# A hybrid decoder layer on one core: inverse RMS moved to the outputs of the up product, with its operands built during a tile-by-tile output projection

## The reference, cut to what matters

```python
h = h + jnp.concatenate([y_conv, y_ret], axis=-1) @ w_out     # 1024 x 1024
hn2 = rmsnorm(h, norm_mlp)                                    # h * rsqrt(mean(h*h)) * gain
h = h + jnp.square(jax.nn.relu(hn2 @ w_up)) @ w_down          # 1024 x 4096, 4096 x 1024
```

## Time and profile before

| | us |
|---|---|
| median of 3 runs (1291.13 to 1292.31) | 1291.59 |
| the profiled execution, its own time | 1291.18 |
| its span, first to last instruction | 1289.4 |
| output projection, 402.9 to 512.3 | 109.4 |
| up product to the start of its last pass, 512.3 to 870.4 | 358.1 |
| last up pass and first down block, 870.4 to 972.5 | 102.1 |
| rest of the down product and the end, 972.5 to 1289.4 | 316.9 |

### The profile page before, as it was taken

One profiled execution on the slowest core, in us unless ns is written; L12 is line 12 of the kernel. 1 busy time (PEld: TensorE's weight loads), 2 busy tenths in 40 slices (PEclk: granted clock), 3 DMA queues, 4 the chain that ended last, 5 costly groups with the idle time before them and its releaser, 6 DMA issues. The chain is left out here.

```text
span 1289.4 us, 22653 instructions
## 1 busy us (share of the span) xinstructions
PE 1172.3 (91%) x8721; PEld 1142.0 (89%) x8721; DVE 730.2 (57%) x1061; ACT 480.7 (37%) x953; POOL 693.1 (54%) x660
## 2 busy tenths in 40 slices
PE   8999999999996998768999999995599999999876
PEld 7889999999996997768999999994499999999875
DVE  4355455455547467964444544443377777777545
ACT  5313214123143333544343434343344444444313
POOL 0144253242423628564646464643488889888972
PEclk9999999999998999879999999998799999999989
DMA  5331311212110543033434343436475455554303
GB/s 183 120 83 50 84 33 51 81 49 67 34 52 18 176 127 99 15 109 108 160 112 152 120 144 128 137 135 190 131 232 147 132 141 156 149 148 133 115 16 117
DMA packets 166125, 142.90 MB, mean 111 GB/s; under 512 B 6140, under 2 KB 133336, under 8 KB 166034
## 3 DMA queue, kind: packets, MB, share of 16 engines
q1 hardware_dynamic: 161262, 139.26, 35.1%
q10 hardware_dynamic: 4772, 2.40, 0.6%
HBM read 101.19 MB, written 40.46 MB: 110 GB/s over the span
## 5 line engine op out<-in xcount | busy, mean ns | idle before, releaser
L1692 PE MATMUL pair<-b_hi,up_hi 128*128 128x258 f32 x896 | 262.0, 292 | 59.0 <-DVE hid L1410 27.3
L1692 PE MATMUL pair<-m_hi,dn_hi 128*128 128x258 f32 x896 | 258.3, 288 | 25.2 <-DVE hid L1473 12.2
L1693 PE MATMUL pair<-b_lo,up_hi 128*128 128x258 f32 x896 | 259.2, 289 | 0.0
L1694 PE MATMUL pair<-b_hi,up_lo 128*128 128x258 f32 x896 | 259.1, 289 | 0.0
L1694 PE MATMUL pair<-m_hi,dn_lo 128*128 128x258 f32 x896 | 256.2, 286 | 0.0
L1693 PE MATMUL pair<-m_lo,dn_hi 128*128 128x258 f32 x896 | 255.7, 285 | 0.0
L1692 PEld LDWEIGHTS pair<-b_hi,up_hi 128*128 128x128 f32 x896 | 175.6, 196 | 63.6 <-issue 34.0
L1692 PEld LDWEIGHTS pair<-m_hi,dn_hi 128*128 128x128 f32 x896 | 172.2, 192 | 27.3 <-issue 14.1
L1499 PE MATMUL pair<-x_hi,w_both 128*128 128x344 f32 (+2 forms) x576 | 189.0, 328 | 0.3 <-DVE v L1128 0.3
L1500 PE MATMUL pair<-x_lo,w_both 128*128 128x344 f32 (+2 forms) x576 | 184.5, 320 | 0.0
L1501 PE MATMUL pair<-x_hi,w_both 128*128 128x344 f32 (+2 forms) x576 | 184.5, 320 | 0.0
(11 more groups left out here) (184 smaller groups left out, 2271.7 us busy)
## 6 DMA issues: line engine op xcount, KB each, us to landing
m_raw<-m_dram SPq DMA_DIRECT2D x56, 516.0 KB, 3.8
m_dram<-hid SPq DMA_DIRECT2D x14, 1548.0 KB, 6.4
up_raw<-w_up_dram SPq DMA_DIRECT2D x32, 512.0 KB, 5.0
dn_raw<-w_down_dram SPq DMA_DIRECT2D x128, 128.0 KB, 2.8
w_raw<-w_in_dram SPq DMA_DIRECT2D x28, 512.0 KB, 3.6
w_raw<-w_out_dram SPq DMA_DIRECT2D x16, 512.0 KB, 4.1
h_dram<-hid SPq DMA_DIRECT2D x16, 258.0 KB, 3.4
h_in<-h_dram SPq DMA_DIRECT2D x16, 258.0 KB, 4.2
```

What stands on the lines that cost most here:

```text
L1692: m_.matmul(to, shs[k], mhs[k], start=STARTS[i] and k == 0, stop=False, skip_group_check=more)
L1693: m_.matmul(to, shs[k], mls[k], start=False, stop=False, skip_group_check=more)
L1694: ins = m_.matmul(to, sls[k], mhs[k], start=False, stop=k == last, skip_group_check=more)
```

## The change

**What moves.** The operands of the up product are built from h times gain alone, without the inverse RMS. The inverse RMS, `r_all`, one row for all partitions, is multiplied to the outputs: DVE's `scaled` does max(x, 0) * r on the four finished blocks of a pass, ACT then only squares them. The relu on ACT goes.

**Output projection.** 16 groups (`SEQ_OUT`) of 48 matmuls, tile by tile over all columns; w_out is loaded and split once. Groups of tiles 0 to 3 take half 0 first, those of 4 to 7 half 1 first. After each group ACT and DVE build what has become complete: `first_block`, `combine` (the four block sums, one tile at a time, on DVE in the place of h itself), `op_split`/`op_rest` (splits tile by tile) and `square_sum` (now on DVE). POOL only adds the residuals, after the split of y (`ylo_done`), and forms sums of weights.

**Up product.** 16 whole passes. `mid_sum` moves from POOL to DVE (ahead of the next pass's step 1); POOL has `up_sum` alone, with a wait of its own for each of the four sums. In pass 0 the last operands (`block_split`/`block_rest` 3 and 5, `op_split`/`op_rest` 6) are built and the inverse RMS is made: row sums on PE after steps 0 and 1, root on one partition, then four transfers (to memory, back as 86 x 12, after the reciprocal to memory again, and to all partitions).

**Crossing to the down product.** `m_raw` lies where `m_lo` goes, one place for each of the seven loads of a block; a load waits for the products that used its place before, no longer for the splits of an earlier load. `mid_split` and `mid_low` stand later in the lists. In SP's list the loads of h stand behind the seven loads of block 0, and the store of the last pass is issued after the first down group's loads.

The core of the diff (waits and placements that the text doesn't speak of are left out):

```diff
-TILES = 2 * KT
-GROUPS = 2 * TILES
+SEQ_OUT = [(n, l) for n in range(KT) for l in ((0, 1) if n < 4 else (1, 0))]
+GROUPS = len(SEQ_OUT)
...
-UP = [(0, (0,)), (1, (0,)), (1, (1,)), (0, (1,))] + [(u, (0, 1)) for u in range(2, UNITS)]
...
+LASTU = UNITS - 1
...
+        m_raw = [[at(f"m_raw{p}_{j}", [2, HALF], F32, mid_place(p, j, 1)) for j in range(7)] for p in range(2)]
...
+            sp.wait_ge(up_sums, 4)
+            sp.wait_ge(up_ready, 4)
             load_up(1)
...
+            for t in range(2):
+                sp.wait_ge(std2_done, t + 1)
+                sp.dma_start(s_dram.rearrange("(l t c) -> t l c", l=2, t=2)[t:t + 1, :, :], std_row[t][0:1, :, :]).then_inc(r_moved, 16)
+            sp.wait_ge(r_moved, 32)
+            sp.dma_start(std_col[0:86, :], s_dram.rearrange("(p c) -> p c", c=12)).then_inc(r_moved, 16)
+            sp.wait_ge(rstd2_done, 1)
+            sp.dma_start(r_dram.rearrange("(p c) -> p c", c=12), std_col[0:86, :]).then_inc(r_moved, 16)
+            sp.wait_ge(r_moved, 64)
+            sp.dma_start(r_all[:, :, :].rearrange("p l c -> p (l c)"), r_dram.unsqueeze(0).to_broadcast([P, COLS - META])).then_inc(r_in, 16)
...
-                if m >= 2:
-                    sp.wait_ge(mid_ready, 2 * m - 2)
+                if b == 0:
+                    sp.wait_ge(up_done, 7 * LASTU + j // 2 + 1)
...
+            for q in range(LASTU):
                 if q:
+                    if q + 1 < UNITS:
+                        sp.wait_ge(up_ready, 7 * q)
+                        load_up(q + 1)
                     store_rest(q - 1)
                 store_first(q)
...
+            sp.wait_ge(up_ready, 7 * UNITS)
+            load_down(0)
+            load_down(1)
             load_mid(0)
             load_mid(1)
+            store_rest(LASTU - 1)
             load_mid(2)
             load_mid(3)
+            load_mid(4)
+            load_mid(5)
+            store_first(LASTU)
+            load_mid(6)
...
             for i in range(4):
                 load_h(0, i)
...
+                if b < BLOCKS - 1:
+                    for j in ((0, 1, 2), (3, 4), (5, 6), ())[n]:
+                        load_mid(7 * (b + 1) + j)
...
+                if wi == 0:
+                    store_rest(LASTU)
...
             pool.wait_ge(main_done, G_OUT)
-            for n in range(4):
+            pool.wait_ge(ylo_done, 4)
+            for n in range(KT):
                 residual(n)
...
+                if u:
+                    pool.wait_ge(up_ready, 7 * (u - 1) + (5, 2, 4, 7)[i])
+                    if u == 1 and i == 1:
+                        pool.wait_ge(r_moved, 32)
...
+            for u in range(1, UNITS):
+                for i in range(4):
+                    up_sum(u, i)
...
+            def squared(q, which):
+
+                act.wait_ge(up_scaled, 4 * q + which + 1)
+                x = (hid_half(0, 0), hid_half(6, 0), hid_half(2, 0), hid_half(3, 1))[which]
+                s.activation(x, x, ACT.Square).then_inc(mid_set, 1)
...
                         if last and j == 17:
-                            y_low(most, 0, 0, 1)
-                            y_low(most, 1, 0, 2)
+                            y_low(most, 0, 1)
+                            y_low(rest, 0, 2)
...
+                if gi >= 2:
+                    square_sum(gi)
+            op_rest(2, 3)
+            up_low(0, 2)
+            combine(4, 3)
             up_low(0, 3)
...
+            def scaled(q, which):
+
+                x = (b11, b22, b21, b12)[which]
+                src = pair[0][:, :, 0:TQ] if q and which == 0 else x
...
+                d.scalar_tensor_tensor(out=x, in0=src, scalar=0.0, in1=r_cols[which % 2], op0=ALU.max, op1=ALU.mult).then_inc(up_scaled, 1)
...
+                    if i == 0 and q:
+                        mid_sum(q - 1)
                     if i == 1:
                         dve.wait_ge(up_done, 7 * q + 2)
...
                         d.tensor_tensor(u2, yb, s1, ALU.add).then_inc(up_read, 1)
+                    if i == 2 and q:
...
+                        scaled(q, 0)
...
+                    if q and i >= 4:
+                        scaled(q, i - 3)
...
+                    if q == 0 and i == 3:
+                        dve.wait_ge(r_moved, 48)
+                        d.reciprocal(std_col[0:86, :], std_col[0:86, :]).then_inc(rstd2_done, 1)
...
+                    if q == 1 and i == 0:
+                        mid_sum(LASTU)
...
+                for t in range(2):
+                    for idx, k in enumerate(K_ORDER):
...
+                        mh, ml = y_hi[:, k, l, TQ * t:TQ * t + TQ], y_lo[:, k, c0 + TQ * t:c0 + TQ * t + TQ]
+                        to = pair[gi % 3][:, t, 0:TQ]
```

More of the change, by code:

```diff
@@ L241, in program @@
[L241 to L250, removed]
+        z0 = rstd_at
@@ L252, in program @@
+        ssq_h = at("ssq_h", [2, HALF], F32, S_LAST)
+        r_all = at("r_all", [2, HALF], F32, S_LAST)
+        b_one = at("b_one", [HALF], F32, S_NEXT)
         up_raw = [at(f"up_raw{s}", [2, KT, P], F32, w + 8192 * (1 - s)) for s in range(2)]
[L253 to L256, removed]
+        o2 = o + 2 * OP
@@ L257, in program @@
+        SLOT = [w2 + 4096 * i for i in range(4)] + [o2 + 4096 * i for i in range(3)]
         up_hi = [at(f"up_hi{i}", [4, P], F32R, SLOT[i]) for i in range(7)]
         up_lo = [at(f"up_lo{i}", [4, P], F32R, SLOT[i] + 2048) for i in range(7)]
[L260 to L264, removed]
@@ L725, in mid_sum @@
[L725 to L736 removed]
+            pool.wait_ge(w_ready, U_OUT + KT)
@@ L1058, in _ @@
+            for q in range(UNITS):
                 for i in range(7):
                     if i == 0:
-                        act.wait_ge(up_done, 7 * q + 1)
-                        if q < 2:
-                            act.wait_ge(normed, 8 if q == 0 else 9)
-                            act.wait_ge(h_saved[q], 16 * KT)
-                        if q:
-                            act.wait_ge(up_read, 5 * (q - 1) + 4)
-                        s.activation(split(hid[:, 0, HALF + c0:HALF + c1]), pair[0][:, tsl, 0:TQ], ACT.Copy).then_inc(up_x_read, 1)
@@ new lines, in _ @@
+                    if q and i in (4, 5):
+                        squared(q, i - 3)
+                    if q == 0 and i == 6:
+                        for which in range(3):
+                            squared(0, which)
+                    if q == 0 and i == 0:
+                        block_split(3)
+                    if q == 0 and i == 2:
+                        block_split(5)
+                    if q == 0 and i == 3:
+                        for k in range(4):
+                            op_split(6, k)
@@ L1307, in head @@
                 if last:
-                    y_low(rest, 0, 0, 3)
-                    y_low(rest, 1, 0, 4)
-                    for l in range(2):
-                        y_low(most, l, 1, 5 + 2 * l)
-                        y_low(rest, l, 1, 6 + 2 * l)
+                    y_low(most, 1, 3)
+                    y_low(rest, 1, 4)
                 assert own[0] == OWN
@@ L1393, in _ @@
-            BLOCK_LOWS = {(1, 2): (0,), (1, 4): (4,), (1, 5): (1,), (1, 6): (2,), (2, 0): (5, 3), (2, 3): (6,)}
-            SCALED = {(0, 4): (0, 1), (0, 5): (2, 3), (0, 6): (4, 5), (1, 1): (6, 7)}
-            for q, (u, ts) in enumerate(UP):
-                c0, c1 = META + TQ * AT[q][0], META + TQ * (AT[q][-1] + 1)
-                tsl = slice(ts[0], ts[-1] + 1)
-                kept = q - 1 if 1 <= q < 4 else q
-                s1, u2, u3, b12 = (split(hid[:, r, HALF + c0:HALF + c1]) for r in range(4))
-                b21, b22 = split(hid[:, 2, c0:c1]), split(hid[:, 6, c0:c1])
-                yb, zb = pair[1][:, tsl, 0:TQ], pair[2][:, tsl, 0:TQ]
+            s1, u2, u3, b12 = (halves(hid_half(row, 1)) for row in range(4))
```

744 lines of the change are left out of this document (360 added, 384 removed).

## The result

| | before | after |
|---|---|---|
| median of 4 runs each, us | 1291.36 | 1219.47 (1217.44 to 1220.61) |
| ratio to before, 95% interval | | 0.9443 (0.9426 to 0.9460) |
| profiled execution, us | 1291.18 | 1217.44 |
| its span, us | 1289.4 | 1215.6 |

The forecast was 1206, the range 1190 to 1240. The profiled execution of the changed kernel is the fastest of its four, 2.0 us under their median.

What follows compares the result with a forecast made beforehand. PE was taken as the bound, its idle time spent waiting for DVE's reads and splits. 403.7 + 93.5 + 49.4 + 267.8 + 73.0 + 316.9 = 1204.3 us of span, plus 1.8 outside it: 1206, range 1190 to 1240.

Steps and rivals of the forecast that it cites:

- up product entered at: Output projection ends at 497.2 us, 15.1 us earlier than before; PE starts the up product 1.2 us after that end.
- passes 0 and 1: First two up passes: 2 x 20.45 us plus 8.5 us of delays (bounds 4 and 20), ending 49.4 us after the projection.
- passes 2 to 14: Steady up passes: the 1.25 us stall for u3 goes, u2 is next; 13 x 20.6 = 267.8 us.
- crossing: Last up pass and first down block: 61.2 us without waits plus 11.8 us of waits, 73 us (bounds 63 and 100).
- rest: Behind the first down block: same matmuls, loads and hand-over as before, so 316.9 us.
- rival C: Output projection: operands are not built in its shadow, so it keeps its 109.4 us; kernel 1221 us, chance 0.06.
- The steady rate: PE's pace in steady up passes: 20.45 us for 168 matmuls without idle time, 0.1217 each.
- the 6.9 and 9.1 of the forecast: DVE and ACT chain from b12 to u2 between passes: 6.9 us alone, 9.1 beside POOL's sums; PE wants u2 after 8.76.
- B: Steady up passes: u2 takes the place of u3, so a pass keeps its 21.7 us; kernel 1220 us, chance 0.12.
- D: Up passes: DVE becomes the bound, a pass up to 30.1 us, kernel up to 1349 us, slower; chance 0.05.
- All sums below use it, at full clock: Whole kernel: the sums price PE's matmuls at 0.1217 us each, as in the steady passes, at full clock.
- Rival A: Crossing to the down product: the transfer queue stays the bound, 27 us more; kernel 1233 us, chance 0.13.

Runs made afterwards that it cites:

- e1: Changed kernel, but POOL no longer waits for the split of y before its residual sums in the projection: 1225.57 us, ratio 0.9496.
- e2: Changed kernel, with the four sums of a pass back on POOL, ahead of its sums of weights: 1248.96 us, ratio 0.9673.
- e3: Changed kernel, with the four sums of a pass back on POOL, behind its sums of weights: 1269.49 us, ratio 0.9830.
- e8: Changed kernel, with one DVE split of weights done three times in passes 2 to 14, just ahead of u2: 1230.34 us, ratio 0.9521.
- e9: Changed kernel, with one DVE split of weights done three times in passes 2 to 14, behind u3: 1219.08 us, ratio 0.9435.
- e6: Changed kernel, with the last pass's four sums spread behind reads of down group 0, not together in group 1: 1217.30 us, ratio 0.9424.
- e13: Changed kernel, with 20, 12 and 20 unread matmuls on PE in three waits (pass 1, pass 15, first down group): 1218.92 us, ratio 0.9427.
- e5: Changed kernel, with the store of pass 14 ahead of the first two loads of its results' block on SP's queue: 1217.58 us, ratio 0.9434.
- e12: Changed kernel with six moves together, reordering loads, sums and splits in passes 0 and 1 and at the crossing: 1210.44 us, ratio 0.9363.
- e7: Changed kernel, with POOL's sums of weights for pass 1 started only after DVE has built operand 5: 1219.18 us, ratio 0.9440.

## Why the prediction was right, and where its sum was off

The direction and the range held; the forecast itself was 13.5 us low, and its own range (1194 to 1218) missed by 1.5. By its terms:

| term | forecast | measured | off by |
|---|---|---|---|
| up product entered at | 498.4 | 497.4 | -1.0 |
| passes 0 and 1 | 48.2 | 53.7 | +5.5 |
| passes 2 to 14 | 267.8 | 266.6 | -1.2 |
| crossing | 73.0 | 75.3 | +2.3 |
| rest | 316.9 | 322.6 | +5.7 |
| span | 1204.3 | 1215.6 | +11.3 |

The other 2.0 us are the profiled execution against its median.

What the change won lies elsewhere in part than where experiments were made. Counted by the matmuls of both traces, of 73.8 us of span 19.8 were won up to the start of the up product, 19.0 in passes 0 and 1 (four half passes before), 13.8 in passes 2 to 14, 22.9 in the crossing, and 1.7 were lost behind it. e1 undoes a part of the first, e2 and e3 the third. That the 19.0 us come from the operands built earlier, and the 22.9 from loads that no longer wait for splits, is read from the waits of PE that are gone, and not shown by a run.

**Projection: right in size, and in cause as far as it was tested.** There is no idle time over 0.4 us within it, and the up product was entered with 0.83 us idle. e1 shows one cause, POOL held back. Building the operands cost nothing, so rival C falls.

**Passes 2 to 14: right.** They took 20.5 us each, and what is left is u2 with 0.3 to 0.5 us, as the forecast named it. The steady rate was a little high: the first two of these passes, in which PE never waits, took 20.17 us and not 20.45. From b12 of a pass to the end of u2 of the next the chain is, with the split and the scaling partly beside POOL:

```profile
714.50 0.70 DVE L1429 TENSOR_TENSOR hid<-pair,hid 128x516 f32<-128x516 f32 x1 [0.92 <-PE pair L1724]
...
716.64 1.77 DVE L1384 SCALAR_TENSOR_TENSOR hid<-hid,r_all 128x516 f32<-128x516 f32 x1
...
722.58 0.69 DVE L1408 TENSOR_TENSOR hid<-pair,hid 128x516 f32<-128x516 f32 x1
```

722.58 + 0.69 - 714.50 = 8.8 us, between the 6.9 and 9.1 of the forecast. e2 shows where the stall came from, e8 and e9 that u2 is next. Rivals B and D fall with them.

**Passes 0 and 1: the waits about right in sum, the clock missing.** The places were operand 5 and u2, plus two of half a microsecond, in all 7.2 us idle (2.83 + 0.41 + 0.51 + 3.49) where the sum had 6.3. That the sum fits is luck in part: step 5 had 0.8 and u2 2.4, both too little, and the other three 3.1, too much. The row sums took 2 x 1.03 us, not 1.0. The inverse RMS was in time: its last transfer was issued at 518.65 and landed 3.3 us later, 25 to 26 us after the projection's end as forecast, and `scaled` took it only at 527.55. The forecast did not count that DVE does the reciprocal only at 516.76, behind operand 5, so this date too is luck in part. The other 3.5 us (53.7 - 2 x 20.45 - 7.2 - 2.1) are the half clock: 0.94 on the mean over 53.7 us is 3.2 lost. "All sums below use it, at full clock" is the step that failed. Rows 1 had shown 0.83 for both stretches with long waits, and I counted that with the waits that go, not with those that stay.

**Crossing: the sum nearly right by luck, its reasons for the most part not.** The forecast had 11.8 us of waits (6 + 2.4 + 3.2, which is 11.6): 6 in group 0 for the first piece of h on the queue, with two splits on DVE ahead of each read, 2.4 in group 1 for a read behind the last four sums, and 3.2 in group 2 for the next piece of h. The second came, at 2.87 us, and e6 shows its cause. The two for h did not: DVE waited for h once, 1.0 us, and PE not at all. In group 0 only the splits on DVE held: PE waited 3.69 us for the copy behind them, and DVE was late with them because it had waited for the store of pass 14 ahead of b22, which cost PE 2.36 us more that the sum did not have. In all that is 8.9 us. The other 5.1 us (75.3 - 61.2 - 8.9) are again half clock (0.93 on the mean over 75.3 us is 5.3 lost), which the sum did not have at all. e13 suggests that this part would not have come back by itself: at a higher clock PE waited for DVE instead. From b22 on DVE is busy 30.25 of 33.3 us. Rival A falls in the form that I gave it; that b22 waits for the queue is a part of it that holds, and e5 shows that its removal alone gains nothing that can be measured.

**The rest: a boundary misread.** I put the end of the first down block of before at 972.5. A block is 4 x 84 = 336 matmuls, and counted in the trace the second block starts at 968.5, so the rest of before was 320.9 us, not 316.9. That is 4.0 of the 5.7. The remaining 1.7 us lie in slightly longer down groups (24 of them take 243.4 us, 242.0 before); no experiment was made on it, and it stays open.

On the contention of DVE and POOL, which three of the experiments turn on: two operations that both read SBUF twice took 1.75 us where they take 0.68 and 1.29 alone. The Trainium skill (SBUF — State Buffer, SBUF: two separate sides) limits this exclusion to VectorE operations with two SBUF inputs, beside those in a two-port mode. The trace agrees for one input: u2 of pass 1, whose other input is in PSUM, ran within a POOL sum at its normal 0.68 us, rows of DVE and POOL in the changed kernel:

```profile
537.15 0.68 DVE L1408 TENSOR_TENSOR hid<-pair,hid 128x516 f32<-128x516 f32 x1
...
536.82 1.53 POOL L670 TENSOR_TENSOR up_s<-up_s,up_raw 128x512 f32<-128x512 f32 x1
```

The POOL sum is longer than 1.29 us, as a split of DVE (two SBUF inputs, 536.09, 1.13 us) was still running at its start.

## What to carry to other kernels

When a wait is removed, ask what its removal starts earlier: five single moves here brought 2 us at most, within their uncertainty, as POOL's sums or the next step in the order took the wait over, and six together brought 9 us. Price a stretch with waits by the clock that its own waits will leave, and check whether another engine would use up the time that a faster PE wins. An engine that is busy 64% of the whole span, as DVE is here, can still be busy 30 of 33 us in one stretch; before work is taken from it, look for a hole in its list, as the 6.55 us ahead of b22, into which other work of its own can move (e12 fits that, but no run shows it alone).

## What the runs showed of the hardware

I had not expected that a wait as short as 1.81 us lowers PE's clock, nor that it does so only sometimes: in e2 the same wait was followed by half clock in seven passes and by full clock in six, a difference of 1.5 us a pass. Behind the 1.25 us of each steady pass before, and behind up to 1.63 us in e8, the clock stayed at 1.00. The other traces bear this out. From the projection on, the 14 traces have 62 waits of PE of 2.9 us and more, and the mean clock over the 4 us behind each of them was below 1.00. Of 87 between 1.8 and 2.9 us 49 were followed by a lower clock, the longest that were not took 2.89 us (e5, e7 and e8). Of 36 between 1.0 and 1.8 us one was, in e12, where the clock had been low ahead of it. What tells the waits in between apart no run shows. With PE busy on matmuls that nobody needs, the clock stayed at 1.00 in the places of the longer waits as well.
